# Neighbourhood attention: two heads' probabilities interleaved key by key, and the meta keys of both turned together

## The reference, cut to what matters

```python
s_loc = jnp.einsum('bhrcd,bhrikd->bhrcik', qg, k_rows) + bias
s_loc = jnp.where(in_win[:, None, :], s_loc, -jnp.inf)
s_meta = jnp.einsum('bhrcd,bmhd->bhrcm', qg, km)
s_all = jnp.concatenate([s_loc.reshape(B, H, R, W, kh * W), s_meta], axis=-1)
p = jax.nn.softmax(s_all, axis=-1)
og = (jnp.einsum('bhrcik,bhrikd->bhrcd', p_loc, v_rows)
      + jnp.einsum('bhrcm,bmhd->bhrcd', p_meta, vm))
sm = jnp.einsum('bqhd,bkhd->bhqk', qm, km)            # meta queries see meta keys only
om = jnp.einsum('bhqk,bkhd->bqhd', jax.nn.softmax(sm, axis=-1), vm)
```

## Time and profile before

| | us |
|---|---|
| median of 3 runs | 1448.64 |
| profiled execution | 1447.95 |
| its span on the core | 1446.1 |
| PE busy | 1425.1 (99%) |
| DVE busy | 810.2 (56%) |
| ACT busy | 560.7 (39%) |
| POOL busy | 543.0 (38%) |

### The profile page before, as it was taken

The page is one execution under the profiler, slowest core; times in us unless marked ns, Lnnn a source line. Parts: engine busy times, 40 slices in busy tenths (PEclk is TensorE's granted clock), DMA queues, the critical chain, the costliest instruction groups (busy, mean ns, idle before and its releaser), DMA issues.

```text
span 1446.1 us, 21210 instructions
## 1 busy us (share of the span) xinstructions
PE 1425.1 (99%) x8912; PEld 1235.0 (85%) x8912; DVE 810.2 (56%) x1169; ACT 560.7 (39%) x885; POOL 543.0 (38%) x232
## 2 busy tenths in 40 slices
PE   9999999999999999999999999999999999999997
PEld 8988887999999999889788777778878888888887
DVE  6933655256666666455799789854463343432023
ACT  6532434453222233323533474564343333333221
POOL 1421211324344344443346333314434443544441
PEclk9999999999999999999999999999999999999999
DMA  7210220212222225876223212112223243332332
GB/s 256 88 59 30 79 79 30 88 53 94 88 96 95 88 93 196 290 266 220 86 90 104 79 68 88 59 46 101 87 74 133 100 146 117 116 101 89 109 109 88
DMA packets 44830, 154.77 MB, mean 107 GB/s; under 512 B 4992, under 2 KB 7808, under 8 KB 44736
## 3 DMA queue, kind: packets, MB, share of 16 engines
q1 hardware_dynamic: 44080, 150.79, 30.4%
q10 hardware_dynamic: 656, 2.62, 0.6%
HBM read 151.17 MB, written 2.10 MB: 106 GB/s over the span
## 4 chain that ended last, share of the span: by engine, by line
PE 89%; DVE 8%; issue 1%; ACT 1%; DMA 0%; SPq 0%; DVEq 0%; ACTq 0%
PE G L538 80%; PE G L855 1%; PE B L816 1%; DVE scb L2373 1%; DVE small L2371 1%; PE B L1143 1%; PE G L763 1%; PE B L1167 1%; PE B L1115 1%; DVE G L1846 1%; DVE kend L1954 0%; PE G L1154 0%; PE B L833 0%; DVE rstd L1876 0%; PE B L508 0%
## 5 line engine op out<-in xcount | busy, mean ns | idle before, releaser
L454 POOL TENSOR_TENSOR wlo<-raw,whi 128x1024 fp32r<-128x1024 f32 x222 | 535.7, 2416 | 880.0 <-ACT whi L1259 880.0
L1259 ACT ACTIVATE whi<-raw 128x1024 fp32r<-128x1024 f32 x224 | 236.6, 1057 | 283.3 <-DMA raw<-wstream 173.2
L538 PE MATMUL G<-xhi,whi 128*128 128x512 f32 (+1 forms) x692 | 273.4, 395 | 2.0 <-DVE xlo L1854 1.8
L538 PE MATMUL G<-xhi,wlo 128*128 128x512 f32 (+1 forms) x692 | 267.2, 386 | 0.0
L538 PE MATMUL G<-xlo,whi 128*128 128x512 f32 (+1 forms) x692 | 267.0, 386 | 0.0
L538 PE MATMUL G<-uhi,whi 128*128 128x258 f32 (+3 forms) x1200 | 258.1, 289 | 4.0 <-DVE ulo L2186 0.8
L538 PE MATMUL G<-uhi,wlo 128*128 128x258 f32 (+3 forms) x1200 | 250.8, 283 | 0.0
L538 PE MATMUL G<-ulo,whi 128*128 128x258 f32 (+3 forms) x1200 | 250.1, 282 | 0.0
L538 PEld LDWEIGHTS G<-uhi,whi 128*128 128x128 f32 x1200 | 189.1, 189 | 16.9 <-issue 13.7
L538 PEld LDWEIGHTS G<-uhi,wlo 128*128 128x128 f32 x1200 | 189.1, 189 | 0.0
L538 PEld LDWEIGHTS G<-ulo,whi 128*128 128x128 f32 x1200 | 188.8, 189 | 0.0
(11 more groups left out here) (363 smaller groups left out, 1692.1 us busy)
## 6 DMA issues: line engine op xcount, KB each, us to landing
raw<-wstream SPq DMA_DIRECT2D x225, 512.0 KB, 3.3
ada_in<-ada SPq DMA_DIRECT2D x40, 512.0 KB, 5.8
ada_late<-ada SPq DMA_DIRECT2D x8, 512.0 KB, 3.6
h<-hT SPq DMA_DIRECT2D x8, 264.0 KB, 3.1
out<-res SPq DMA_DIRECT2D x8, 256.0 KB, 2.5
biasn<-bias SPq DMA_DIRECT2D x2, 960.0 KB, 8.1
biasn<-bias ACTq DMA_DIRECT2D x2, 960.0 KB, 4.7
scan_keep<-scanm SPq DMA_DIRECT2D x1, 528.0 KB, 7.2
```

Source lines behind the costliest of these rows:

```text
L454: pool.tensor_tensor(wlo[:, i, :], raw[:, i, :], whi[:, i, :].bitcast(F32), ALU.subtract)\
L538: ins = pe.matmul(dst[:, x, 0:xw], w[:, slot, b * P:(b + 1) * P], u[:, k, off + x0:off + x0 + xw], start=(first and i == 0 and j == 0), st ...
L1259: act.activation(whi[:, m % RING, :], raw[:, m % RING, :], ACT.Copy).then_inc(s["unit_hi"], 1)
```

## The change

`sc` keeps its bytes, but the two heads' columns alternate: key n of head 0, key n of head 1, key n+1 of head 0, and so on. Seen by one head, the columns are 8 bytes apart. The 16 meta keys of both heads are then 32 neighbouring columns, which one transpose turns to 32 partitions (2n + head). It goes to bank 2 alone. So there is one meta transpose per stage in place of two, the last of the stage, and ACT's copy (bank 2, with the meta keys) waits for it, while DVE's copy (bank 3) waits only for the body and is 128 columns shorter. For the values, the meta rows of `vna`'s tile 4 hold head 0's tokens in even rows and head 1's in odd rows, with zeros in between; they come from a small buffer `vrows` (32 columns, half of them zero for each head's partitions), which `evac_columns` fills with two instructions of 64x16 in place of one of 128x16. With a single `vrows`, the evacuation of v tile 1 also waits for the turn of v tile 0. The meta queries' own probabilities are interleaved in the same way: 4 transposes and 4 products of two heads in place of 8 and 8. `small` is 128 bytes larger, and all that lies behind it moves up by 128 bytes.

```diff
--- before.py
+++ after.py
@@ -168,7 +168,7 @@
         vec = sb("vec", [P, NVEC], at); at += -(-4 * NVEC // 64) * 64
         ident = sb("ident", [P, P], at); at += 512
         ones = sb("ones", [P, P], at); at += 512
-        small = sb("small", [P, 160], at); at += 640
+        small = sb("small", [P, 192], at); at += 768
         A0 = -(-at // 64) * 64
 
         def arena(offset):
@@ -186,6 +186,8 @@
         rs = small[:, 88:96]
         rinv = small[:, 96:104]
         top8 = small[:, 112:120]
+        vrows = small[:, 160:192]
+        vpair = vrows.rearrange("p (n a) -> p a n", a=2)
         row_sum = small[:, 120:136].rearrange("p (b h) -> p b h", b=2)
 
 
@@ -232,13 +234,14 @@
         gmask = sb("gmask", [P, 2, P], arena(o), I32); o += 1024
 
         S = sb("S", [P, 2, NCHUNK, 2, DV], arena(GATES))
-        sc = sb("sc", [P, 3, 2, 400], arena(GATES))
+        sc2 = sb("sc", [P, 3, 800], arena(GATES))
+        sc = sc2[:, :, :].rearrange("p b (n a) -> p b a n", a=2)
         pt = sb("pt", [P, 2, 2, 512], arena(GATES + 9600))
         metok = sb("metok", [META, 512], arena(GATES + 17792))
         rbn = sb("rbn", [P, 8, DH], arena(GATES + 23232))
         rbs = sb("rbs", [P, 512], arena(GATES + 25280))
         msc = sb("msc", [META, P], arena(GATES + 19840))
-        mpt = sb("mpt", [META, P], arena(GATES + 20352))
+        mpt = sb("mpt", [2 * META, P], arena(GATES + 20352))
 
         yhi = sb("yhi", [P, JF, SEQ], arena(128), F32R)
         ylo = sb("ylo", [P, JF, SEQ], arena(45184), F32R)
@@ -799,7 +802,7 @@
                 pe.wait_ge(s["evac_done"], T0["mixed"] + MIXED.index(("v", hp)) + 1)
                 for i in range(4):
                     pe.transpose(B4[:, 2, i * P:(i + 1) * P], vT[:, hp % 2, META + P * i:META + P * (i + 1)], ident[:, :])
-                pe.transpose(B4[0:META, 3, 0:P], vT[:, hp % 2, 0:META], ident[:, :]).then_inc(s["vna_ps"], 1)
+                pe.transpose(B4[0:2 * META, 3, 0:P], vrows, ident[:, :]).then_inc(s["vna_ps"], 1)
 
             def na_scores(st):
                 hp, a = st // 4, st % 4
@@ -830,10 +833,11 @@
                 for par in range(2):
                     pe.wait_ge(s["na_p"], 2 * st + par + 1)
                     for b in range(nb):
-                        pe.transpose(B4[:, 2 + par, b * P:(b + 1) * P],
-                                     sc[:, st % 3, par, body + b * P:body + (b + 1) * P], ident[:, :])
-                    pe.transpose(B4[0:META, 2 + par, nb * P:(nb + 1) * P], sc[:, st % 3, par, meta:meta + META], ident[:, :])\
-                        .then_inc(s["na_t_ps"], 1)
+                        last = pe.transpose(B4[:, 2 + par, b * P:(b + 1) * P],
+                                            sc[:, st % 3, par, body + b * P:body + (b + 1) * P], ident[:, :])
+                last.then_inc(s["na_t_ps"], 1)
+                pe.transpose(B4[0:2 * META, 2, nb * P:(nb + 1) * P], sc2[:, st % 3, 2 * meta:2 * (meta + META)], ident[:, :])\
+                    .then_inc(s["na_t_ps"], 1)
 
             def na_values(st):
                 hp, a = st // 4, st % 4
@@ -853,7 +857,7 @@
                     for par in range(2):
                         hh = 2 * hp + par
                         last = pe.matmul(G[par * DH:(par + 1) * DH, 1, hp % 2, a * P:(a + 1) * P],
-                                         vna[:, tile, hh * DH:(hh + 1) * DH], pt[:, st % 2, par, b * P:(b + 1) * P],
+                                         vna[:, tile, hh * DH:(hh + 1) * DH], pt[:, st % 2, par if b < nb else 0, b * P:(b + 1) * P],
                                          start=(b == 0), stop=(b == nb))
                 last.then_inc(s["na_o_ps"], 1)
 
@@ -904,17 +908,16 @@
                     last.then_inc(s["meta_s_ps"], 1)
                 if st == 13:
                     pe.wait_ge(s["meta_e"], 1)
-                    for hh in range(NA_H):
-                        last = pe.transpose(B4[0:META, 3, P + hh * META:P + (hh + 1) * META],
-                                            msc[:, hh * META:(hh + 1) * META], ident[0:META, 0:META])
+                    for hp in range(4):
+                        last = pe.transpose(B4[0:2 * META, 3, P + hp * META:P + (hp + 1) * META],
+                                            msc[:, 2 * META * hp:2 * META * (hp + 1)], ident[0:META, 0:META])
                     last.then_inc(s["meta_t_ps"], 1)
                 if st == 14:
                     pe.wait_ge(s["meta_pt"], 1)
                     pe.wait_ge(s["evac_done"], T0["w_o"])
-                    for hh in range(NA_H):
-                        i = 4 * (hh % 2) + hh // 2
-                        last = pe.matmul(G[0:META, 0, 0, hh * DH:(hh + 1) * DH], mpt[:, i * META:(i + 1) * META],
-                                         vna[0:META, 4, hh * DH:(hh + 1) * DH], start=True, stop=True)
+                    for hp in range(4):
+                        last = pe.matmul(G[0:META, 0, 0, hp * P:(hp + 1) * P], mpt[:, hp * META:(hp + 1) * META],
+                                         vna[0:2 * META, 4, hp * P:(hp + 1) * P], start=True, stop=True)
                     last.then_inc(s["meta_o_ps"], 1)
                 if st == 16:
                     meta_turn()
@@ -1467,7 +1470,7 @@
                 act.activation(vna[:, 0:4, hp * P:(hp + 1) * P], B4[:, 2, :].rearrange("p (a n) -> p a n", a=4), ACT.Copy)
                 if hp == 0:
                     act.wait_ge(s["amat_done"], 1)
-                act.activation(vna[0:META, 4, hp * P:(hp + 1) * P], B4[0:META, 3, 0:P], ACT.Copy).then_inc(s["vna_done"], 1)
+                act.activation(vna[0:2 * META, 4, hp * P:(hp + 1) * P], B4[0:2 * META, 3, 0:P], ACT.Copy).then_inc(s["vna_done"], 1)
 
             def na_exp(st):
                 hp, a = st // 4, st % 4
@@ -1484,7 +1487,7 @@
             def na_pt_evac(st):
 
                 nb = na_window(st % 4)[1] // 16
-                act.wait_ge(s["na_t_ps"], 2 * st + 1)
+                act.wait_ge(s["na_t_ps"], 2 * st + 2)
                 if st >= 2:
 
                     act.wait_ge(s["na_o_ps"], st - 1)
@@ -1530,7 +1533,7 @@
                 if st in (5, 9, 13):
                     vna_evac((st - 1) // 4)
                 if st == 13:
-                    act.activation(mpt[:, :], B4[0:META, 3, P:2 * P], ACT.Copy).then_inc(s["meta_pt"], 1)
+                    act.activation(mpt[:, 0:4 * META], B4[0:2 * META, 3, P:P + 4 * META], ACT.Copy).then_inc(s["meta_pt"], 1)
                 if st in (14, 15):
 
                     act.wait_ge(s["unit_used"], U0["w_o"])
@@ -2006,7 +2009,12 @@
                 body = dst[:, META:T].rearrange("p (c x r) -> p x r c", x=2, r=4)
                 scale = rstd1[:, META:T].rearrange("p (x r c) -> p x r c", x=2, r=4)
                 dve.wait_ge(s["tile_half"], i - 3)
-                dve.tensor_tensor(dst[:, 0:META], bank[:, 0, 0:META], rstd1[:, 0:META], ALU.mult)
+                if MIXED[i][0] == "v":
+                    for x in range(2):
+                        rows = slice(DH * x, DH * (x + 1))
+                        dve.tensor_tensor(vpair[rows, x, :], bank[rows, 0, 0:META], rstd1[rows, 0:META], ALU.mult)
+                else:
+                    dve.tensor_tensor(dst[:, 0:META], bank[:, 0, 0:META], rstd1[:, 0:META], ALU.mult)
                 if MIXED[i][0] == "k":
                     dve.tensor_tensor(dst[:, T:T + META], bank[:, 0, 0:META], rstd1[:, 0:META], ALU.mult)
                 dve.tensor_tensor(body[:, 0], bank[:, 0, META:META + SEQ // 2].rearrange("p (r c) -> p r c", r=4),
@@ -2025,8 +2033,8 @@
                     dve.wait_ge(s["unit_used"], U0["mixed"] + i + 1)
                     normed(sg[:, m, :], G[:, MIXED_BUF[i]])
                 elif kind == "v":
-                    if m >= 2:
-                        dve.wait_ge(s["vna_ps"], m - 1)
+                    if m >= 1:
+                        dve.wait_ge(s["vna_ps"], m)
                     evac_columns(i, vT[:, m % 2, :])
                 else:
                     evac_columns(i, (qna if kind == "q" else kna)[:, m, :])
@@ -2049,6 +2057,7 @@
                 after_piece(13 + i)
             dve.wait_ge(s["gmask_in"], 16)
             dve.memset(vna[:, 4, :], 0.0)
+            dve.memset(vrows, 0.0)
             link(dve.memset(Amat[:, :, :], 0.0))
             for i in range(5):
                 n = P if i < 4 else META
@@ -2094,11 +2103,11 @@
 
             def na_pt_copy(st):
                 nb = na_window(st % 4)[1] // 16
-                dve.wait_ge(s["na_t_ps"], 2 * st + 2)
+                dve.wait_ge(s["na_t_ps"], 2 * st + 1)
                 if st >= 2:
 
                     dve.wait_ge(s["na_o_ps"], st - 1)
-                dve.tensor_copy(pt[:, st % 2, 1, 0:(nb + 1) * P], B4[:, 3, 0:(nb + 1) * P]).then_inc(s["na_pt1"], 1)
+                dve.tensor_copy(pt[:, st % 2, 1, 0:nb * P], B4[:, 3, 0:nb * P]).then_inc(s["na_pt1"], 1)
 
             def na_inverse(hp):
 
@@ -2139,12 +2148,13 @@
                 if st == 13:
 
```

(12 more changed lines are left out.)

## The result

The changed kernel takes 1454.93 us (median of 6 runs, 1453.88 to 1455.62); the kernel before, over all six of its runs, 1448.16. The ratio is 1.0052, 95% interval 1.0042 to 1.0062 (the two medians alone give 1.0047): slower by half a per cent. The forecast was 1446.8 with a range up to 1454.0, so it missed, by size and by sign. The profiled execution is 1455.49 us with a span of 1453.4, 7.3 us more than before.

A forecast was written before the change was run, and what follows sets the result against it. The prediction took PE, busy for 99% of the span, to bound the kernel. Its terms, -1.09 - 0.11 - 0.14 - 0.64 + 0.18 = -1.80 us, took 1448.64 to 1446.84 us, with a range of 1445.4 to 1454.0.

The forecast's parts named there:

- The step that failed: After the attention: nothing waits for a clock of its own, so the whole -1.80 us shift reaches the end.
- +0.09 (v tile 0): Ahead of stage 0: PE waits 0.09 us longer for v tile 0's evacuation, half of the +0.18 term.
- Transposes that go: Stages 1 to 13: 0.109 us per meta transpose, -1.09 and -0.11 us in all; swallowed by waits in stages 1 and 9.
- The stride: Accesses to `sc` with 8 bytes between a head's columns: no extra cost, 0 us, on DVE, ACT and weight loads.
- the rival with 0.95 ns per column: Rival on weight loads: 14 ns on each of 80 transposes, +1.1 us, so 1447.9; chance 0.16 together with another case.
- The extra instruction of the v evacuation: Two small DVE instructions for one per v tile: 0.09 us each, PE waiting at tiles 0 and 2, +0.18 us.
- L916: Meta queries' products: 8 records of twice the width instead of 16, about 0.5 us of 0.99 saved, counted within the tail.
- the tail's term of 0.64: Stages 14 to 17, DVE-bound: 0.38 us from an earlier start plus 0.26 from two shorter copies of pt, -0.64 us.
- ACT's later copy: ACT's copy of pt waits two or three transposes longer, 0.22 to 0.33 us, but is covered: 0; uncovered +0.9 us.
- weight loads at half rate: Rival: the stride makes each body transpose 0.218 us for 0.109, net +5.8 us, so 1454.4; chance 0.12.
- DVE at the far-stride price: Rival: 0.9 ns more per element on DVE's scale and maximum, net +5.4 us, so 1454.0; chance 0.11.

The follow-up runs named there:

- shift128: The kernel before with only `small` 128 bytes larger, every buffer behind it 128 bytes higher, no instruction changed: 1455.04 us, ratio 1.0055.
- inter_packed: The changed kernel with vrows in free columns of `small`, so `small` and every other buffer keep their old places: 1447.4 us, ratio 1.0002.
- load4byte: The packed kernel with its 80 body transposes loading neighbouring columns of kna (4 bytes apart) instead of probabilities, values wrong: attention 112.85 us against 113.54.
- masked: The packed kernel with `small` 256 bytes larger than before and a v tile's meta columns written by one 128x32 instruction instead of two: 1446.75 us, ratio 0.9996.
- packed kernel: Another name for inter_packed: the changed kernel with vrows in free columns of `small`, buffers in their old places: 1447.4 us, ratio 1.0002.
- shift64: The kernel before with only `small` 64 bytes larger: 1450.73 us, ratio 1.0021.
- shift256: The kernel before with only `small` 256 bytes larger: 1447.37 us, ratio 1.0001.
- all128: The kernel before with every buffer on chip 128 bytes higher, weight ring included: 1447.3 us, ratio 1.0001.
- weights128: The kernel before with the weight ring and what lies up to `small` 128 bytes higher, `small` packed, everything behind in its old place: 1465.6 us, ratio 1.0127.
- both128: The kernel before with the weight ring and everything behind it 128 bytes higher, while h, uhi, ulo, xhi and xlo stay: 1459.38 us, ratio 1.008.
- y0: The kernel before with only yhi and ylo moved, by -128 bytes: 1452.3 us, ratio 1.0033.

## Why the prediction was wrong

**The step that failed** is the last one of the sum: "After the attention nothing waits for a clock of its own: weights are prefetched on buffers that PE frees, so the shift reaches the end." The reasoning looked at waits alone. What changed was the length of 1284 matmuls whose instructions are the same and whose operand had moved. The description of the change said that all behind `small` moves up by 128 bytes, and the prediction gave that move no line and no price, not even as a rival. It is worth +7.7 us, against -0.74 for everything that the prediction did price; shift128 (+7.7) and inter_packed (no change) show the two apart, and 7.7 less 0.74 is 7.0, near the 6.8 between the medians.

The other terms were off too. Of the forecast -1.80, one +0.09 (v tile 0) lies ahead of the attention's first landmark, which leaves -1.89 for the attention; -0.74 came:

- Transposes that go: 0.109 us each was right for what they cost before, and the two places where it is swallowed (stages 1 and 9) are where PE waits longer now (0.5 to 0.6 us, and 0.49 to 0.85).
- The stride, taken at 0: DVE paid nothing, which was right. ACT paid: its exponential went from 621 to 662 ns for 400 elements and from 514 to 536 for 272, so from 0.84 to 0.98 ns per element between the two lengths; no run shows what that alone costs in time. The weight load paid 0.120 for 0.109 us per transpose, 0.69 us in all by load4byte. This is the rival with 0.95 ns per column; its size (14 ns per transpose, +1.1 us) was near. Its reason (a price per 16 bytes touched) was not: 16 bytes cost what 8 do.
- The extra instruction of the v evacuation: the term was 0.09 us per tile; it is 0.28 (201.01 to 201.38 against 201.03 to 201.12), and masked gave 0.25 of it back in the attention.
- L916: taken at half, it is unchanged. The analogy was with L855, whose matmuls fill two halves of the result's partitions by turns and start 0.07 us apart; those of L919 all have the same 16 partitions as result. There the time went with the columns: 0.062 us for 64, 0.121 for 128. That the alternating halves are what makes L855 cheaper is not shown. With it the tail's term of 0.64 was too high: from PE's start at 237.43 (now 237.33) to the last values it is 9.21 us before and 8.93 after, 0.28 less.
- ACT's later copy: taken at 0. PE's matmuls show no wait for ACT's pt, but the weight loads do, 0.6 us that they did not have before (the PEld row of the packed kernel above; before, their idle time was for issue and ACT's sc). The sum below leaves little room for a cost, but no run takes this wait out.

Put together: 0.69 for the stride, 0.19 for the small instruction in stage 9 and 0.36 for the tail are 1.24, and -1.89 for the attention plus 1.24 is -0.65, near the -0.74 measured. The two large rivals of the stride (weight loads at half rate, DVE at the far-stride price) did not happen, although the time came near theirs by chance: 1454.4 and 1454.0 against 1454.9. Had only the time been looked at, either would have seemed confirmed; the rows of L836 (0.120) and L2098 (0.99) rule out both.

The Trainium skill ("Advanced Engine Details and Errata", SBUF Cachelines) would have an 8-byte stride free and a 16-byte one not. DVE and its 8 bytes agree (991 before, 0.99 us after). TensorE's weight load does not: 8 and 16 bytes both give a mean LDWEIGHTS of 207 and 209 ns against 140 for neighbours, and the same step between transposes. Nor quite does ACT (621 to 662 ns at 8 bytes). The measurements decide.

## What to carry to other kernels

A change that makes a buffer larger moves everything allocated behind it, and that move is an edit of its own with a price: list the addresses of the operands that the hottest matmuls read, before and after. Here the ring of fp32r weights and the streamed operand have to begin alike modulo 256 bytes; grow the buffer by a multiple of 256 bytes, or put the new columns into free ones. Either only avoids the loss: neither repaired version is shown to be faster than the kernel before (ratios 1.0002 and 0.9996). When the time comes out wrong, group the instructions by operand and shape first: a few ns on every instruction of one operand is a cause that no list of waits shows.

## What the runs showed of the hardware that was not expected

- A 128x128 by 512 fp32r matmul takes about 6 ns more (389 to 395 in the records, 4 to 5 for xhi and xlo) when weights and streamed operand begin 128 bytes apart modulo 256, and 0 more at 0 or 256 bytes apart; at 64 bytes it is 5, 3 or -1 ns by which of the three products it is. For the 258-column products on uhi, whose operand begins 48 or 56 bytes apart already, the ring's move gives 285 for 284 ns. Why the place counts is open.
- An ACT exponential over columns 8 bytes apart takes 662 ns for 400 elements, 621 over neighbours.
- Two DVE instructions on 64 partitions each delay the next one on 128 by 0.37 us, one on 128 partitions by 0.09 to 0.10.
- In the changed kernel's profile the granted clock falls in the GLA part. From 130 to 140 us (PE, PEld, DVE, ACT and POOL busy, then the clock), first before, then after:

```profile
130.00:140.00 10.00, 9.76 (x81) 8.99 (x80) 1.36 (x3) 5.17 (x11) 2.40 (x1) 1.00 0.16 52
```
```profile
130.00:140.00 10.00, 10.00 (x70) 9.31 (x69) 1.65 (x4) 4.50 (x11) 2.38 (x1) 0.83 0.17 52
```

From 120 to 130 us, ahead of the fall, PE is busy for all of the 10.00 us in both kernels. At the lower of its levels, 1.2 GHz, a matmul of 256 columns starts 0.21 us after the last instead of 0.12. What brings it about was not tried. It does not explain the loss: the profiles of shift128, shift64, shift256 and all128, all with the old instructions, have 0.83 there as well, and the last two are as fast as the kernel before, while inter_packed, weights128, both128, y0 and masked have 1.00. It lies ahead of the attention, which began only 0.37 us later in the changed kernel. (Before, the clock also falls once PE has done its last matmul: 0.56 from 1440 to 1446 us, so it is full throughout only while PE works.)
